# A layer with expert retrieval on one core: scores of the first token tile copied straight into the search buffers, fewer heads scored ahead of the gathers, the second half's scores kept in SBUF, and VectorE summing rows from slot 3 on

## What is computed

```python
def chunk(yb):                                     # 128 tokens; 8 heads, 128 keys, top 16
    q = (yb @ w_q).reshape(PEER_CHUNK, PEER_HEADS, 2, PEER_HALF)
    s = jnp.einsum('chpk,hpnk->chpn', q, sub_keys)
    s1, i1 = lax.top_k(s[:, :, 0], PEER_TOPK)
    s2, i2 = lax.top_k(s[:, :, 1], PEER_TOPK)
    cand = (s1[..., :, None] + s2[..., None, :]).reshape(..., PEER_TOPK * PEER_TOPK)
    sc, ci = lax.top_k(cand, PEER_TOPK)
    idx = row * PEER_KEYS + col                    # one of 16384 experts
    gate = jax.nn.softmax(sc, axis=-1)
    act = jax.nn.gelu(jnp.einsum('ched,cd->che', u[idx], yb), approximate=False)
    return jnp.einsum('che,ched->cd', gate * act, v[idx])
```

## Time and profile before

| | |
|---|---|
| median of 3 runs | 3590.55 us (3589.64 to 3593.45) |
| profiled execution | 3589.91 us |
| its span | 3588.1 us, 1.8 us less than its own time |
| granted TensorE clock, mean | 0.965 |
| busy: PE, DVE, ACT, POOL | 84%, 65%, 35%, 38% |
| first gather, last product | 583.6 us, 3571.4 us |

### The profile page before, as it was taken

One profiled execution on the slowest core, in us unless ns is written; L12 is line 12 of the kernel. 1 busy time (PEld: TensorE's weight loads), 2 busy tenths in 40 slices (PEclk: granted clock), 3 DMA queues, 4 the chain that ended last, 5 costly groups with the idle time before them and its releaser, 6 DMA issues.

```text
span 3588.1 us, 30319 instructions
## 1 busy us (share of the span) xinstructions
PE 3021.1 (84%) x8472; PEld 1466.3 (41%) x8472; DVE 2320.3 (65%) x5783; ACT 1266.0 (35%) x3609; POOL 1366.7 (38%) x1236
## 2 busy tenths in 40 slices
PE   6998879989999999976989799997777777777776
PEld 5776664434444444432433344442222222222222
DVE  4333343656777989785876766666776666667664
ACT  3444221332454545542222333333333333333332
POOL 3333300342434443443443443334444444444442
PEclk9999889999999999988999899999999999999999
DMA  4221225999988999889999999999999999999997
GB/s 151 86 74 58 100 76 189 405 409 386 369 326 323 367 342 357 331 312 414 398 419 367 353 421 421 420 421 419 415 419 414 416 416 417 414 414 416 419 415 321
DMA packets 199673, 1221.14 MB, mean 340 GB/s; under 512 B 22864, under 2 KB 31056, under 8 KB 68176
## 3 DMA queue, kind: packets, MB, share of 16 engines
q0 software_dynamic: 147456, 1073.81, 74.3%
q1 hardware_dynamic: 51040, 145.25, 10.9%
q10 hardware_dynamic: 1008, 0.14, 0.0%
HBM read 1193.42 MB, written 25.69 MB: 340 GB/s over the span
## 4 chain that ended last, share of the span: by engine, by line
PE 50%; DMA 31%; DVE 8%; ACT 4%; issue 4%; SPq 2%; POOL 2%; POOLq 0%; DVEq 0%; ACTq 0%
DMA ring<-uv,idx 27%; PE r_o L1616 21%; PE w_ps L1357 10%; PE w_ps L1387 7%; PE w_ps L1598 5%; DVE ring L1312 4%; DMA w_raw<-w_in 1%; DMA s<-s_scr 1%; PE w_ps L1566 1%; PE w_ps L1440 1%; POOL ring L613 1%; ACT diag L876 1%; PE w_ps L1459 1%; SPq L405 1%; PE r_o L1440 1%
## 5 line engine op out<-in xcount | busy, mean ns | idle before, releaser
L1616 PE MATMUL r_o<-ring,diag 128*128 128x512 f32 x3684 | 1774.6, 617 | 419.4 <-ACT diag L876 393.6
L613 POOL DMA_INDIRECT ring<-uv,idx x1024 | 1159.3, 1132 | 1817.4 <-PE r_o L1616 1668.7
L1312 DVE CUSTOM_DVE_ANT_0 ring<-ring,ytok 128x1024 f32<-128x1024 f32 x1024 | 1251.7, 1222 | 641.4 <-DMA ring<-uv,idx 633.3
L1616 PEld LDWEIGHTS r_o<-ring,diag 128*128 128x128 f32 x3684 | 680.6, 194 | 1398.9 <-issue 752.0
L863 ACT ACTIVATE gel<-dot 128x2 f32<-128x2 f32 x512 | 104.0, 203 | 1601.8 <-DVE dot L1312 1601.2
L1387 PE MATMUL w_ps<-x_raw,w_raw 128*128 128x512 f32 x704 | 325.2, 595 | 1.2 <-DMA w_raw<-w_in 1.2
L876 ACT ACTIVATE diag<-ident,coef 128x128 f32<-128x128 f32 x921 | 318.9, 387 | 15.0 <-PE r_o L1616 15.0
L1357 PE MATMUL w_ps<-xh,wb 128*128 128x512 f32 x704 | 246.2, 415 | 22.0 <-POOL wb L567 14.4
L1598 PE MATMUL w_ps<-yT,wq 128*128 128x512 f32 x512 | 251.8, 598 | 3.1 <-DMA wq<-wq 2.4
L867 ACT ACTIVATE coef<-gel,gate 128x1 f32<-128x1 f32 x1024 | 246.0, 287 | 16.8
L1387 PEld LDWEIGHTS w_ps<-x_raw,w_raw 128*128 128x128 f32 x704 | 130.8, 192 | 149.0 <-issue 147.0
(11 more groups left out here) (181 smaller groups left out, 2613.3 us busy)
## 6 DMA issues: line engine op xcount, KB each, us to landing
w_raw<-w_in SPq DMA_DIRECT2D x88, 512.0 KB, 3.5
wq<-wq SPq DMA_DIRECT2D x32, 512.0 KB
ring<-uv,idx POOLq DMA_INDIRECT x1024
wc_raw<-w_branch SPq DMA_DIRECT2D x16, 768.0 KB, 9.0
wo_raw<-w_out SPq DMA_DIRECT2D x16, 512.0 KB, 22.9
s_scr<-s_out SPq DMA_DIRECT2D x16, 512.0 KB
s<-s_scr SPq DMA_DIRECT2D x64, 128.0 KB
x_raw<-xT SPq DMA_DIRECT2D x16, 256.0 KB, 7.3
```

The source lines that it names most:

```text
L613: nc.gpsimd.indirect_dma_start(out=ring[t % RING][:], out_offset=None, in_=a["uv"], in_offset=bass.IndirectOffsetOnAxis(ap=idx[:, slot:slo ...
L1312: nc.vector.tensor_tensor_reduce(ring[r][:, 0:D], ring[r][:, 0:D], ytok[n % 2][:], 1.0, 0.0, ALU.mult, ALU.add, dot[:, slot:slot + 1]).the ...
L1616: ins = nc.tensor.matmul(o_ps[n % 2][half][:], diag[(u - 1) % DIAGS][:], ring[t % RING][:, D + half * HALF:D + (half + 1) * HALF], start=s ...
```

## The change

Four parts. **(1)** In stage 0, ACT copies tile 0's scores of each head from PSUM straight into the search buffer `s` (semaphore `s_direct`), and then all four tiles to `s_out` as before; the 8 loads back for tile 0 are gone, and SP's queue ahead of slot 0 ends with the load of `ytok`. **(2)** HEAD_LEN[0] goes from 14 to 10 and SCORES_AT[0] from -69 to -28: heads 0 and 1 and most of head 2 stand ahead of slot 0, heads 3 to 7 follow at 10 slots each, to slot 52. `compare` and `scores_out` are generators of their own, so that a compare stands in the middle of the next query block and not behind it. The search of head 2 starts at slot 6 (LATE_STEPS). **(3)** In stage 1 the scores go to a buffer `s_all` in SBUF that holds all heads and tiles; the 8 stores and 32 loads back are gone; SCORES_AT[1] goes from 443 to 461, so scoring ends at slot 589. **(4)** `by_vector` takes the odd slots from 3 on in tile 0 (48 more) and, with the later SCORES_AT[1], 4 more in tile 3. The exponents move from the 13th to the 15th slot of a head, `invert` and `share` to the 2nd and 3rd of the next.

```diff
+LATE_STEPS = [2 if 6 <= j < 15 else 0 for j in range(TOPK)]
-HEAD_LEN = (14, 16)
-SCORES_AT = (-69, 443)
+HEAD_LEN = (10, 16)
+SCORES_AT = (-28, 461)
 def by_vector(t):
-    if not 24 <= t % SLOTS < SLOTS - 4 or t % 2 == 0:
+    if not (24 if t >= SLOTS else 3) <= t % SLOTS < SLOTS - 4 or t % 2 == 0:
         return False
-    return step_at(1, 0) <= t < branch_at(1, 0) or (branch_at(1, 0) <= t < score_at(1, 0) and t % 4 == 1)
+    return t < branch_at(1, 0) or (branch_at(1, 0) <= t < score_at(1, 0) and t % 4 == 1)
...
+    s_all = at("s_all", 0, [P, RH, GT, 2 * NK])
...
         advance = woven(stage_chain(stage))
-        for h in range(3):
-            advance(stored_at(0, h))
-            search_in(h)
+        advance(-1)
         tokens_in(0)
         for slot in range(LAST_SLOT):
...
-            if slot % TOPK == 6 and k + 3 < RH * TT:
+            if slot % TOPK == 6 and RH <= k + 3 < RH * GT:
                 search_in(k + 3)
...
+        def scores_out(g):
+            half = HEAD_LEN[g] // 2
+            for h in range(RH):
+                for p in range(2):
+                    hp = HP * g + 2 * h + p
+                    yield score_at(g, h) + half * p + half + 2
+                    act.wait_ge(scored, hp + 1)
+                    bank = ps[2 + hp % 2]
+                    if g == 0:
+                        if h >= SBUFS and p == 0:
+                            act.wait_ge(s_used, h - SBUFS + 1)
+                        nc.scalar.activation(s[h % SBUFS][:, p], bank[:, 0:NK], ACT.Copy).then_inc(s_direct, 1)
+                        if h >= 2 and p == 0:
+                            act.wait_ge(s_stored[h % 2], 16 * (h // 2))
+                        dst = s_out[h % 2][:, :, p * NK:(p + 1) * NK]
+                    else:
+                        dst = s_all[:, h, :, p * NK:(p + 1) * NK]
+                    nc.scalar.activation(dst, bank[:].rearrange("p (t n) -> p t n", t=GT),
+                                         ACT.Copy).then_inc(s_copied, 1)
...
-            dve.wait_ge(s_in[g % SBUFS], 16 * (g // SBUFS + 1))
+            if g < RH:
+                dve.wait_ge(s_direct, 2 * g + 2)
+            elif g < RH * GT:
+                dve.wait_ge(s_in[g % SBUFS], 16 * ((g - RH) // SBUFS + 1))
+            else:
+                dve.wait_ge(s_copied, HP + 2 * h + 2)
...
-                if slot == 22 and n in BASED:
+                if slot == (22 if n else 0) and n in BASED:
                     lay_base(n)
...
-                    for _ in range(STEPS_AT[slot % TOPK]):
+                    for _ in range((LATE_STEPS if g == LEAD else STEPS_AT)[slot % TOPK]):
                         next(search)
...
+        def compares(g):
+            part = HEAD_LEN[g] // 2
+            for i in range(HP):
+                hp = HP * g + i
+                yield score_at(g, i // 2) + part * (i % 2 + 1) + 1
```

More of the change, by code:

```diff
@@ L232, in build @@
     kT = [at(f"kT{g}", (12, 32)[g], [P, HP, NK]) for g in range(NG)]
-    s_out = [[at(f"s_out{g}{r}", (20, 0)[g] + 4 * r, [P, GT, 2 * NK]) for r in range(2)] for g in range(NG)]
+    s_out = [at(f"s_out{r}", 20 + 4 * r, [P, GT, 2 * NK]) for r in range(2)]
+    s_all = at("s_all", 0, [P, RH, GT, 2 * NK])
     st_a = at("st_a", 104, [P, 32])
@@ L815, in rest @@
             turned(GT - 1)
[L817 to L822, removed]
-                                     ps[2 + hp % 2][:].rearrange("p (t n) -> p t n", t=GT),
-                                     ACT.Copy).then_inc(s_copied, 1)
             half = HEAD_LEN[g] // 2
@@ L835, in rest @@
                     nc.scalar.activation(qT[g][hp % 2][:], ps[hp % 2][:], ACT.Copy).then_inc(q_copied, 1)
-                    if hp % HP:
-                        yield score_at(g, h) + half * p + half + 1
-                        scores_out(hp - 1)
-            yield score_at(g, RH) + half + 1
-            scores_out(HP * (g + 1) - 1)
+        def scores_out(g):
[6 more added lines that the diff above has]
+                    bank = ps[2 + hp % 2]
+                    if g == 0:
+                        if h >= SBUFS and p == 0:
[8 more added lines that the diff above has]
+                                         ACT.Copy).then_inc(s_copied, 1)
         def stage(g):
-            return merged(units(g), pooling(g), exponents(g), turned_out(g), head_norm(g), rest(g))
+            return merged(units(g), pooling(g), exponents(g), turned_out(g), head_norm(g), rest(g), scores_out(g))
         def exponent(g):
@@ L897, in _ @@
                 g = RH * n + slot // TOPK + LEAD
-                if slot % TOPK == 12 and g < RH * TT:
+                if slot % TOPK == 14 and g < RH * TT:
                     exponent(g)
@@ L1153, in retrieve @@
             h = g % RH
-            rows = s[g % SBUFS]
+            rows = s[g % SBUFS] if g < RH * GT else s_all[:, h, g // RH - GT].rearrange("p (a b) -> p a b", a=2)
             steps = iter(range(PER * g + 1, PER * (g + 1) + 1))
@@ L1339, in _ @@
                         search = retrieve(g)
-                    for _ in range(STEPS_AT[slot % TOPK]):
+                    for _ in range((LATE_STEPS if g == LEAD else STEPS_AT)[slot % TOPK]):
                         next(search)
-                    if slot % TOPK == 14:
-                        invert(g)
-                    if slot % TOPK == 15:
-                        share(g)
+                if slot % TOPK == 1 and LEAD < g <= RH * TT:
+                    invert(g - 1)
+                if slot % TOPK == 2 and LEAD < g <= RH * TT:
+                    share(g - 1)
                 if n:
@@ L1573, in rest @@
             turn(GT - 1)
-            def compare(hp):
-                pe.wait_ge(q_copied, hp + 1)
-                if hp % HP >= 2:
-                    pe.wait_ge(s_copied, hp - 1)
-                for j in range(GT):
-                    ins = nc.tensor.matmul(ps[2 + hp % 2][:, j * NK:(j + 1) * NK], qT[g][hp % 2][:, j * P:(j + 1) * P],
-                                           kT[g][:, hp % HP, :], start=True, stop=True)
-                ins.then_inc(scored, 1)
             part = HEAD_LEN[g] // 2
@@ L1600, in rest @@
                     ins.then_inc(q_unit, 1)
-                    if hp % HP:
-                        compare(hp - 1)
-            yield score_at(g, RH) + part
-            compare(HP * (g + 1) - 1)
+        def compares(g):
[3 more added lines that the diff above has]
+                yield score_at(g, i // 2) + part * (i % 2 + 1) + 1
+                pe.wait_ge(q_copied, hp + 1)
+                if i >= 2:
+                    pe.wait_ge(s_copied, hp - 1)
+                for j in range(GT):
+                    ins = nc.tensor.matmul(ps[2 + i % 2][:, j * NK:(j + 1) * NK], qT[g][i % 2][:, j * P:(j + 1) * P],
+                                           kT[g][:, i, :], start=True, stop=True)
+                ins.then_inc(scored, 1)
         def stage(g):
-            return merged(units(g), pooling(g), scores(g), turns(g), values(g), outs(g), rest(g))
+            return merged(units(g), pooling(g), scores(g), turns(g), values(g), outs(g), rest(g), compares(g))
         def spread(n, slot):
```

29 lines of the change are left out of this document (12 added, 17 removed).

## The result

The changed kernel takes 3534.14 us (3530.01 to 3534.79, 4 runs) against 3592.0 us (3589.64 to 3594.58, 4 runs) of the kernel before: 0.9836 of it, 95% interval 0.982 to 0.9851, 58 us less. 3554 was forecast, in a range of 3538 to 3574. The direction was right.

The account below looks back on a forecast made before the run. DMA bytes were taken to bound most stretches, PE some, with a chain of query blocks ahead of the first gather. Terms 9.6 + 6.6 + 5 + 6 + 9 = 36 us off 3589.9 gave 3554 us, range 3538 to 3574.

Parts of the forecast that it names:

- The first gather: Start of stage 0: earlier compare and direct copy bring the first gather from 583.62 to 574.0 us, 9.6 us earlier.
- The wait ahead of the first product: Tile 0's first product waits for `ytok`, queued behind head 2's load back; it moves from 616.13 to 593 us.
- The hole: Idle DMA behind the first gathers, 9.6 us, mostly closes; 3 us left, 6.6 us gained.
- The weighed rule: Round-robin between queues gives SP about half the bandwidth: wq and `ytok` in 5 us, 1 to 2 us less in the sum.
- The sums: Slots 3 to 98, half the rows on VectorE: gain only in slots 84 to 96, 5 us, at most 7.5.
- While scoring: Stage 1's scoring without stores and loads back: 6 us, between 0 and 14; PE's busy time allows at most 7.
- The new wait that was feared: Second half: a head's search may wait for ACT's copy of its second half-score, holding the next product and the ring.
- Behind the scoring: From slot 589 to the end, DMA full: 26 loads back of 0.35 us go, 9 us, not below 5.
- The exponents: Exponents, invert and share moved within a head, same instructions, waits 14 slots ahead of the gates' use: nothing.
- The signs: Expected profile: product of slot 84 16 us earlier, slot 96 21 earlier, no window below share 0.9 from 580 to 645.
- (b): Rival: VectorE becomes the bound in slots 3 to 98, 33 us lost and the 5 not gained: 3592 us; chance 0.09.
- (d): Rival: scoring gives its 14 us, slots 84 to 99 their 7.5, the hole closes wholly: 3537 us; chance 0.06.

Follow-up runs that it names:

- e4: The changed kernel with stage 0's scoring at its old places (14 slots a head from slot -69), direct copies kept: 3544.39 us, ratio 0.9864.
- e11: The changed kernel with tile 0's `ytok` load issued behind the last store of y, ahead of the query weights: 3525.66 us, ratio 0.9817.
- e10: The kernel before with only the new sums (odd slots 3 to 97 of tile 0 on VectorE): 3576.27 us, ratio 0.996.
- e2: The changed kernel without its new sums on VectorE in tile 0: 3574.94 us, ratio 0.9951.
- e9: The kernel before with part 3 alone (`s_all`, no stage 1 stores and loads back), scoring still from slot 443: 3573.09 us, ratio 0.9945.
- e5: The changed kernel with stage 1's score stores and loads back issued again, into buffers nobody reads: 3560.55 us, ratio 0.9908.
- e6: The changed kernel with stage 1's scoring from slot 443 instead of 461: 3535.8 us, ratio 0.9841.
- e7: The kernel before with only the exponents moved late (15th slot, invert and share in the next head): 3589.87 us, ratio 0.9991.
- e3: The changed kernel with exponents, invert and share back at their old places, head 2 apart: 3539.87 us, ratio 0.9856.

## Why the prediction was right, and where it was not

- **The first gather: right.** 9.6 us forecast, 41.4 - 31.8 = 9.6 measured, for the reason given.
- **The wait ahead of the first product: read wrongly.** The prediction has tile 0's first product wait for `ytok`. In the kernel before it followed VectorE's wait of 10.96 us for ACT's exponents, and e4 shows the same wait at 31.66 us. It is the fewer blocks ahead of slot 0, and with them the earlier exponents, that bring the first product forward; only then does `ytok` become what is waited for, 7.3 us in the changed kernel. The text named the blocks beside `ytok`, so the sum did not suffer by it.
- **The hole: `ytok`'s landing mis-sized, and the size of the term met by luck.** 10 us were taken and 14.11 measured; 3 us of the hole were to be left, and 7.9 were. From the first gather to slot 64 the gain is 6.0 us against 6.6 all the same, but mostly by a higher rate of full DMA engines from 645 us on (421 GB/s for 411), which was not forecast. The weighed rule (each DMA engine goes round-robin between queues, packet by packet; the Trainium skill, DMA: Bandwidth & Descriptors, Queues, rings and completion order) gave 5 us. The trace does not agree with half of the bandwidth: from 581.8 to 595.9 us SP's queue moved 1.57 MB of 5.85, 27%. It had 432 of the profile's 1017 packets, 42%, and they were half as large as the gathers'. e11 shows what the step was worth: 6 to 8 us.
- **The sums: a step that failed.** "From slot 84 to 96 PE was full" was read rightly, but the price stopped at slot 96. PE's backlog lasts to slot 112: with the sums as the only edit (e10) the 12 slots to 96 gain 7.0 us and the 16 behind them 7.2. In the changed kernel slots 64 to 128 gain 9.1 instead of 5, since 6.8 are lost ahead of slot 84. And the text treated the sums as cover for the start only in passing: without them the whole change is worth 17 us and not 58 (e2).
- **While scoring: the step that failed by most.** 6 us taken, 13.8 measured. The cap of 7 us was what PE's busy 345.87 us left of 353. That busy time is modelled from overlapping matmuls and did not bound the stretch: with fewer bytes the 128 slots of scoring took 343.4 us (e9) and 342.8 (changed kernel), PE then busy for nearly all or all of it, 11.5 and 12.1 less than the 354.9 of before. The rest of the gain lies in the 18 slots outside the scoring, where the cap did not hold. The upper bound of the text, 14 us by SP's queue's price, was the right figure. e5 and e9 show that bytes are what it was, e6 that the place was not. The new wait that was feared is 1.6 us in all, over 3 times, in the answer on VectorE's first step of a search:

```profile
  ACT s_all L840: 1.6, 3
```

- **Behind the scoring: right.** 9 us forecast, 8.1 to 9.5 measured.
- **The exponents: put at nothing, worth 2 (e7) to 6 us (e3).** "Same instructions" was true, but VectorE's 13 waits of `invert` for ACT, 11.2 us, were in the trace of before and weren't looked for. They are the only cause found of the 7.1 us in slots 128 to 443; how much of it they are stays open, since e5, without these waits, gains only 0.4 there, and e10, with them, 4.2.
- **The signs.** The product of slot 96 came 21.1 us earlier, as forecast (21), but that of slot 84 only 10.2 and not 16. The window from 600 to 616 us has a DMA share of 0.56, where none was to be below 0.9. The gathers' issue took 40.38 / 35 = 1.15 us from 645 to 745 us, now with sums on VectorE, against 1.07 in the earlier trace rows: most of the step to 1.31 that was laid to the sums belongs to something else in that stretch.

```profile
645.00:745.00 100.00, 40.38 (x35) 0.98 1.01 422
```

- **The rivals.** (b), VectorE as the bound, did not come: 2.85 us a slot over slots 0 to 64. (d), more of everything, is nearest, with 0.06 and 3537 us: scoring did give its 14 and the slots behind 84 more than their 7.5, but the hole did not close, and the 7 us behind slot 128 were in none of the rivals.

## What to carry to other kernels

Do not cap a gain by an engine's modelled busy time: 347.77 us of busy PE before became 342.8. Counted instructions times their start-to-start distance, 344.3, came nearer, and even that is an estimate. Where an engine is full at the end of a stretch, follow its backlog into the next stretch before the price stops. Where two resources are near their bound at once (here PE and the DMA engines from slot 0 to 128), price an edit together with the others: sums alone gave 17 us, without them the rest gave 17, together 58. And a load that gates a whole stage belongs ahead of the traffic that fills the DMA engines; here one moved load of 512 KB was worth 6 to 8 us.

## What the runs showed of the hardware

A 512 KB load issued while 8 gathers of 1 MB were in flight landed after 14.11 us, and its queue moved 27% of the bytes meanwhile. PE's clock: idle for 13.4 us, then four rows of spread in 3.78 us instead of 1.72, that is at the lower of its two levels, 1.2 of 2.4 GHz, with a granted clock of 0.50 from 600 to 603.8 us:

```profile
600.00:603.80 3.80, 3.75 (x5) 1.69 (x6) 3.53 (x8) 0.29 (x1) 0.00 (x0) 0.50 0.05 22
```

Behind 5.89 us of idle in e11 the four rows took 3.78 us too. Fourteen profiled executions, of kernels whose edits all lie behind the start of the first query block, reached it between 540.2 and 544.6 us, so a single profile tells no effect under 4 us unless it is counted from the place where the kernels begin to differ.
